# Moving half of the second tile's one-hot building from VectorE to GpSimd in a decoder layer's expert stage

## The reference, cut to what matters

```python
def eval_block(args):
    xb, eb, wb = args                     # tokens, expert numbers, softmax weights
    u = peer_u[eb]
    a = jax.nn.gelu(jnp.einsum('td,tkd->tk', xb, u), approximate=False)
    return jnp.einsum('tk,tkd->td', wb * a, peer_v[eb])
...
h = layer_norm(ALPHA * h + ffn, ln2_g[l], ln2_b[l])
```

## Time and profile before

| what | value |
|---|---|
| median of 3 runs | 2379.71 us (2378.01 to 2379.8) |
| the profiled execution: its own time | 2377.85 us |
| its span, first to last instruction | 2376.1 us |
| mean granted TensorE clock | 0.903 |
| PE, DVE, ACT, POOL busy | 83%, 68%, 37%, 40% |
| dots of `peer_u` with tile 0's placing | about 1525 to 1825 us |
| tile 1's placing | about 1826 to 1879 us |
| panels and row additions | about 1879 to 2356 us |
| layer norm and output | the rest |

### The profile page before, as it was taken

The page is one execution under the profiler, slowest core; times in us unless marked ns, Lnnn a source line. Parts: engine busy times, 40 slices in busy tenths (PEclk is TensorE's granted clock), DMA queues, the critical chain, the costliest instruction groups (busy, mean ns, idle before and its releaser), DMA issues.

```text
span 2376.1 us, 30754 instructions
## 1 busy us (share of the span) xinstructions
PE 1965.3 (83%) x10815; PEld 1624.4 (68%) x10815; DVE 1608.1 (68%) x2290; ACT 872.2 (37%) x1485; POOL 954.0 (40%) x559
## 2 busy tenths in 40 slices
PE   8999999999999999999953333264546899999996
PEld 8899999998889988887952222254445666666663
DVE  7444455554444555556989999999997866666666
ACT  6444434344444444446431212378675500000000
POOL 0000000000000000000258888888884288888884
PEclk9999999999999999999986657676666999999998
DMA  7544465556555565543989999999998399999997
GB/s 242 162 139 141 147 198 176 188 170 202 189 187 190 179 194 187 185 160 128 375 327 403 421 421 419 412 420 412 416 419 325 128 411 412 411 411 411 411 410 285
DMA packets 213889, 678.50 MB, mean 286 GB/s; under 512 B 14713, under 2 KB 64257, under 8 KB 180225
## 3 DMA queue, kind: packets, MB, share of 16 engines
q0 software_dynamic: 57664, 394.31, 40.8%
q1 hardware_dynamic: 156112, 282.75, 35.6%
HBM read 674.89 MB, written 2.11 MB: 285 GB/s over the span
## 4 chain that ended last, share of the span: by engine, by line
PE 48%; issue 22%; POOL 11%; DMA 9%; DVE 8%; ACT 1%; DVEq 0%; another core or an unknown queue 0%; POOLq 0%; ACTq 0%; SPq 0%
PE ps L449 47%; POOL v_rows L1875 8%; DMA u_rows<-in_peer_u,idx_all 8%; POOL u_rows L1862 3%; DVE junk L1655 2%; DVE ohs L1688 1%; DMA v_rows<-in_v_gathered,idx_all 1%; DVE ohs L1685 1%; DVE h L1703 0%; ACT hi L908 0%; DMA raw<-in_peer_wq 0%; DVE ki L1615 0%; DVE pos L1628 0%; DVE ki L1608 0%; DVE pos L1625 0%
## 5 line engine op out<-in xcount | busy, mean ns | idle before, releaser
L1296 DVE TENSOR_TENSOR lo<-raw,hi 128x1024 fp32r<-128x1024 f32 x368 | 448.7, 1225 | 483.3 <-ACT hi L908 482.6
L1862 POOL DMA_INDIRECT u_rows<-in_peer_u,idx_all x256 | 537.5, 2100 | 175.3 <-issue 68.6
L908 ACT ACTIVATE hi<-raw 128x1024 fp32r<-128x1024 f32 x376 | 397.3, 1059 | 566.7 <-PE ps L449 560.1
L1655 DVE SCALAR_TENSOR_TENSOR junk<-u_rows,h 128x2048 bf16<-128x2048 f32 x226 | 514.9, 2281 | 30.7 <-DMA u_rows<-in_peer_u,idx_all 28.7
L449 PE MATMUL ps<-v_raw,wt 128*128 128x368 f32 x1536 | 475.4, 472 | 2.6 <-DMA v_raw<-in_peer_v 1.8
L1875 POOL DMA_INDIRECT v_rows<-in_v_gathered,idx_all x256 | 393.5, 1537 | 144.1 <-issue 126.5
L449 PE MATMUL ps<-xh,hi 128*128 128x256 f32 (+2 forms) x1536 | 438.9, 286 | 1.2 <-issue 0.9
L449 PE MATMUL ps<-xh,lo 128*128 128x256 f32 (+2 forms) x1536 | 435.1, 283 | 0.0
L449 PE MATMUL ps<-xl,hi 128*128 128x256 f32 (+2 forms) x1536 | 434.4, 283 | 0.0
L1703 DVE SCALAR_TENSOR_TENSOR h<-v_rows,coef_all,h 128x944 f32<-128x944 f32 x256 | 307.7, 1202 | 172.1 <-DMA v_rows<-in_v_gathered,idx_all 170.4
L449 PEld LDWEIGHTS ps<-v_raw,wt 128*128 128x128 f32 x1536 | 291.6, 190 | 186.0 <-DMA v_raw<-in_peer_v 2.7
(11 more groups left out here) (234 smaller groups left out, 2517.1 us busy)
## 6 DMA issues: line engine op xcount, KB each, us to landing
raw<-in_w_in SPq DMA_DIRECT2D x96, 1024.0 KB, 5.3
v_raw<-in_peer_v SPq DMA_DIRECT2D x128, 552.0 KB
raw<-in_w_in SPq DMA_DIRECT2D x64, 256.0 KB, 3.2
raw<-in_w_in SPq DMA_DIRECT2D x32, 512.0 KB, 4.9
raw<-in_p_a SPq DMA_DIRECT2D x16, 1024.0 KB, 5.1
raw<-in_p_b SPq DMA_DIRECT2D x16, 1024.0 KB, 5.1
raw<-in_w_o SPq DMA_DIRECT2D x16, 1024.0 KB, 5.0
raw<-in_peer_wq SPq DMA_DIRECT2D x16, 1024.0 KB, 10.2
```

The source lines that it names most:

```text
L908: return nc.scalar.activation(o, i, f, **kw)
L1296: V.tensor_tensor(raw_lo[:, hh // 2, k4, :] if kept else lo[:, hh % SLOT_N, :, :], raw[:, hh // 2, k4, :], (kept_hi(hh) if kept else hi[:, ...
L1655: V.scalar_tensor_tensor(junk[:, n % 2, :], u_rows[row_slot(u, k)][:, :], 1.0, h1[:, u // PH, :], ALU.mult, ALU.mult, accum_out=dots[:, u ...
L1862: Q.indirect_dma_start(u_rows[slot][:, :], None, peer_u, bass.IndirectOffsetOnAxis(ap=idx_all[:, n:n + 1], axis=0)).then_inc(u_in[slot], 16)
```

## The change

Tile 1's second keys leave VectorE. GpSimd makes them, in 4 instructions of 128 for each chunk (`second_key`, new), for 3 chunks of 4; ScalarE keeps the fourth, which is now the one with `c % 4 == 2`. VectorE makes first keys alone, and reads the numbers 0 to 127 from a copy in PSUM bank 5, beyond the columns of a panel. Tile 1's keys are transposed and copied ahead of the last coefficient, which follows alone. `tile_open` is cut into its six products: five stand behind chunks 36 to 40, and the last, whose bank holds VectorE's numbers, behind chunk 63. `gather_v(3)` stands amid GpSimd's keys and `gather_v(4)` behind the last `tile_open`. The scaling of tile 1's sum (`scale_acc(1)`) moves into the additions.

```diff
-ACT_B = 3
+ACT_B = 2
+OPEN_AT = 4
...
+        def pool_keys(c):
+            return sum(n % 4 != ACT_B for n in range(CHUNKS_T, c))
+        iota_ps = ps[:, 5, CW:CW + P]
...
             def place(c):
...
                     if c % 4 == ACT_B:
                         pe.wait_ge(S("oh_ready"), CHUNKS_T + (c - CHUNKS_T) // 4 + 1)
+                    else:
+                        pe.wait_ge(S("oh_pool_ready"), pool_keys(c + 1))
...
+            slots_turn(1, (1, 2))
             pe.wait_ge(S("dots_done"), 2 * PH * TOPK)
-            slots_turn(1)
-            for T in range(NT):
-                tile_open(T)
+            slots_turn(1, (0,))
             for c in range(CHUNKS_T, 2 * CHUNKS_T):
                 place(c)
+                n = c - CHUNKS_T - OPEN_AT
+                if 0 <= n < NT * len(CUTS) - 1:
+                    tile_open(n // len(CUTS), n % len(CUTS))
+            pe.wait_ge(S("oh_dve_ready"), CHUNKS_T)
+            tile_open(NT - 1, len(CUTS) - 1)
...
+            slots_copy(1, (1, 2), 2)
             gelu(2 * PH - 1)
-            slots_copy(1)
+            slots_copy(1, (0,), 3)
+            act.wait_ge(S("slots_copied"), 2)
             key_one_hots(CHUNKS_T + ACT_B)
...
-            def one_hots(c):
+            def first_key(c):
                 dve.wait_ge(S("w_done"), c - OHR + 1)
-                o = oh[c % OHR]
                 t0 = c % CHUNKS_T * WB
-                if c % 4 != ACT_B:
-                    V.tensor_tensor(o[:, 1, :, :], iota[:, :].unsqueeze(1).to_broadcast([P, WB, P]),
-                                    slots_t[:, 2, t0:t0 + WB].unsqueeze(2).to_broadcast([P, WB, P]), ALU.is_equal)
                 for q in range(WB):
-                    ins = V.tensor_scalar(o[:, 0, q, :], iota[:, :], slots_t[:, 1, t0 + q:t0 + q + 1],
+                    ins = V.tensor_scalar(oh[c % OHR][:, 0, q, :], iota_ps, slots_t[:, 1, t0 + q:t0 + q + 1],
                                           slots_t[:, 0, t0 + q:t0 + q + 1], ALU.is_equal, ALU.mult)
...
-            scale_acc(1)
-            dve.wait_ge(S("slots_copied"), 2)
+            V.tensor_copy(iota_ps, iota[:, :]).then_inc(S("iota_copied"), 1)
+            dve.wait_ge(S("iota_copied"), 1)
+            dve.wait_ge(S("slots_copied"), 3)
             for c in range(CHUNKS_T, 2 * CHUNKS_T):
-                one_hots(c)
+                first_key(c)
...
+            def second_key(c):
+                pool.wait_ge(S("w_done"), c - OHR + 1)
+                t0 = c % CHUNKS_T * WB
+                for q in range(WB):
+                    ins = Q.tensor_scalar(oh[c % OHR][:, 1, q, :], iota[:, :], slots_t[:, 2, t0 + q:t0 + q + 1], None,
+                                          ALU.is_equal)
+                ins.then_inc(S("oh_pool_ready"), 1)
+
+            for n in range(3):
+                gather_v(n)
+            pool.wait_ge(S("slots_copied"), 2)
+            for c in range(CHUNKS_T, 2 * CHUNKS_T):
+                if c % 4 != ACT_B:
+                    second_key(c)
+                if c == CHUNKS_T + 16:
+                    gather_v(3)
+            pool.wait_ge(S("tile_opened"), 2)
+            for n in range(4, NT * SLOTS):
                 gather_v(n)
```

More of the change, by code:

```diff
@@ L803, in h1_turn, with tile_open @@
                     last.then_inc(S("h1t_turned"), 1)
-            def tile_open(T):
-                for n, (a, b) in enumerate(CUTS):
-                    last = mm(ps[:, 3 * T + n, 0:b - a], alpha_i[:, :], h1[:, T, a:b], True, False)
-                last.then_inc(S("tile_opened"), 1)
+            def tile_open(T, n):
+                a, b = CUTS[n]
+                last = mm(ps[:, 3 * T + n, 0:b - a], alpha_i[:, :], h1[:, T, a:b], True, False)
+                if n == len(CUTS) - 1:
+                    last.then_inc(S("tile_opened"), 1)
             def dots_pair(u):
@@ L843, in dots_pair, with slots_turn @@
                     products(b)
-            def slots_turn(T):
-                pe.wait_ge(S("coef_ready"), PH * (T + 1))
+            def slots_turn(T, parts):
                 pe.wait_ge(S("topk_done"), PH * (T + 1))
+                if 0 in parts:
+                    pe.wait_ge(S("coef_ready"), PH * (T + 1))
                 if T:
@@ L852, in slots_turn @@
                     pe.wait_ge(S("h1t_copied"), 8)
-                for n, src in enumerate((coef_all[:, T, :], ij_all[:, T, 0, :], ij_all[:, T, 1, :])):
-                    last = nc.tensor.transpose(ps[:, 6, n * P:(n + 1) * P], src, ident[:, :])
+                for n in parts:
+                    src = ij_all[:, T, n - 1, :] if n else coef_all[:, T, :]
+                    bank = 7 if T and n == 0 else 6
+                    last = nc.tensor.transpose(ps[:, bank, n * P:(n + 1) * P], src, ident[:, :])
                 last.then_inc(S("slots_turned"), 1)
@@ L877, in _ @@
                 if u == PH:
-                    slots_turn(0)
+                    slots_turn(0, (0, 1, 2))
                 if u >= PH:
@@ L1210, in pair_copies, with slots_copy @@
                     A(ut[:, g % 2, :], ps[:, 3 + g % 2, :], ACT.Copy).then_inc(S("ut_copied"), 1)
-            def slots_copy(T):
-                act.wait_ge(S("slots_turned"), T + 1)
-                A(slots_t[:, :, :].rearrange("p a t -> p (a t)"), ps[:, 6, 0:3 * P], ACT.Copy
-                  ).then_inc(S("slots_copied"), 1)
+            def slots_copy(T, parts, count):
+                act.wait_ge(S("slots_turned"), count)
+                bank = 7 if parts == (0,) else 6
+                A(slots_t[:, parts[0]:parts[-1] + 1, :].rearrange("p a t -> p (a t)"),
+                  ps[:, bank, parts[0] * P:(parts[-1] + 1) * P], ACT.Copy).then_inc(S("slots_copied"), 1)
             def one_hots(c):
@@ L1269, in _ @@
                 if u == PH:
-                    slots_copy(0)
+                    slots_copy(0, (0, 1, 2), 1)
                     act.wait_ge(S("slots_copied"), 1)
@@ L1740, in _ @@
             coefs(2 * PH - 1)
[L1742 to L1743 removed]
+            V.tensor_copy(iota_ps, iota[:, :]).then_inc(S("iota_copied"), 1)
+            dve.wait_ge(S("iota_copied"), 1)
+            dve.wait_ge(S("slots_copied"), 3)
             for c in range(CHUNKS_T, 2 * CHUNKS_T):
[L1745 removed]
+                first_key(c)
             for n in range(NT * SLOTS):
+                if n == SLOTS // 2:
+                    scale_acc(1)
                 add_row(n)
@@ L1870, in gather_v @@
                 elif n == 3:
-                    pool.wait_ge(S("tile_opened"), 2)
+                    pool.wait_ge(S("tile_opened"), 1)
                 elif n == 5:
@@ L1892, in _ @@
                     gather_u(u, k)
-            for n in range(NT * SLOTS):
+            def second_key(c):
[15 more added lines that the diff above has]
+            for n in range(4, NT * SLOTS):
                 gather_v(n)
```

2 lines of the change are left out of this document (1 added, 1 removed).

## The result

| | median | runs | ratio to before, 95% interval |
|---|---|---|---|
| before | 2379.02 us | 6 (2376.92 to 2379.8) | |
| with the change | 2387.32 us | 6 (2386.55 to 2389.3) | 1.0037 (1.0026 to 1.0047) |

The change makes the kernel 8.3 us slower, by the interval 6 to 11 us.

A forecast was written before the change was run, and what follows sets the result against it. TensorE's panels and the full stream of gathers bound the end. Panels start 2.1 us earlier, but the late opening and row cost 1.8 us: -0.3 us, 2379.71 to 2379.4 us, no measurable change; range 2376 to 2388.

The forecast's parts named there:

- the slower rival with GpSimd as the pace: Tile 1's placing: GpSimd paces it; at 0.60 us an instruction +11 us, 2390.7 us; 17%, of which 5% stay within 0.2%.
- Part 2: Turn of four chunks: GpSimd at 0.35 us an instruction hides, ScalarE's key one-hots come next; 5.74 us against 5.9.
- The high end: GpSimd's key instruction: upper price of 600 ns, from another operation's 3.15 ns a column.
- ScalarE's order as the next limit: Placing turn: ScalarE's key one-hots for chunk c + 2 stand behind the copy of chunk c; a turn is 5.74 us.
- The start: Start of the placing: chunk 32 placed at about 1827.9, 3.3 us earlier, part going back to the lower clock.
- The tail: Behind the last placing: sixth opening delays gathers 0.62 us, gather 4's row adds 1.2 us; together 1.8 us.
- The blocking at the end: First additions meeting chunk 63's keys on the port lock, one addition 1.2 us; put at 0, 0.5 us in the range.
- The rival of a lock for PSUM reads: Placing: the lock holds for PSUM reads too, so VectorE and GpSimd serialise; about +26 us, 2406 us; 4%.
- The rival of a clock that does not rise: Placing: TensorE's work is thinner at the start, placings twice as long, a turn about 3 us longer; +20 us, 2400; 4%.

The follow-up runs named there:

- prices: Kernel before, with 16 GpSimd instructions added at its start, where neither VectorE nor GpSimd has other work; equality with a pointer scalar on 128 columns took 0.585 us.
- half_keys: Changed kernel with 2 of GpSimd's 4 instructions for each chunk left out (keys of every second token not built); 2380.39 us, ratio 1.0006.
- open_amid: Kernel before with only its six openings moved behind chunks 36 to 41, one-hots made as before; 2376.53 us, ratio 0.999.
- late_row: open_amid with the sixth opening behind chunk 63 and gather 4 behind it; 2377.17 us, ratio 1.0002.
- numbers_sbuf: Changed kernel with VectorE's first keys reading the numbers from SBUF and not from PSUM; 2385.82 us, ratio 1.004.

## Why the prediction was wrong, step by step

The time lay inside the range (2376 to 2388), on the side of the slower rival with GpSimd as the pace and 0.7 us below the bound; the forecast of no change was wrong.

- **The step that failed is Part 2, GpSimd's price.** It was taken as 0.35 us an instruction, "near the cast, because it has the same width and one input too". It is 0.58 us, by itself as in the placing. The high end that stood beside it, 0.60 us from the slope of the other operation, was right within 4%. The rival built on it gave 1887.4 us for the last placing (measured 1886.55) and +11 us (measured +11.4 between the traces, +8.3 between the medians). That it came so close is partly luck: it took 2.5 us a chunk, and with the 2.32 us that were measured its own sum gives 1829.9 + 22 x 2.32 + 2.5 = 1883.4. The other 3.2 us are two things that it did not have, the additions' hold on the last keys (2.4 us) and a last placing at the lower clock (1.95 us for 1.13). The slope of that end, 3.15 ns a column, stands beside 2.7 measured in prices; the cast's likeness in width and inputs says nothing of what an equality costs.
- **What follows next.** ScalarE's order as the next limit was right (5.93 us a turn by half_keys, 5.74 predicted), and so was the consequence that the pace would hardly change even with a cheap GpSimd.
- **The start** was right: first placing at 1827.76 (1827.9), first keys from PSUM 0.32 us apart, chunk 36 ended at 1834.69 + 1.13 = 1835.82 (1835.7). That the clock takes part of the earlier start back was right too; open_amid's trace shows the same by itself.
- **The tail** was about right: 1.8 us for the late opening and the late row, against 2.9 in the change's one trace, 1.5 in late_row, and 2.1 between the means of the seven traces with them and the seven without.
- **The blocking at the end** was put at 0, and cost 2.4 us of GpSimd's last keys (and 2.0 us of its first eight, which the first placing did not feel). The range had 0.5 us for it. The margin that was to hide it (2.70 us that chunk 62 waits for ScalarE) existed only while GpSimd was not the limit itself.
- The rival of a lock for PSUM reads did not come; nor did the full exclusion for SBUF reads that numbers_sbuf tested. VectorE's 128 first keys from PSUM took 401 to 413 ns in the change, beside a full GpSimd. The rival of a clock that does not rise did not come either: it was 1.00 from 1837 to 1847.
